# Conv-FFN stage of a streaming encoder layer on one core: first adds ahead of weight splits, normalising spread over two periods, token loads moved at block changes

## The reference

```
up = h @ w_up                       # 1024 -> 2 x 2816
ext = concat([conv_hist, up])
c = ext[0:T]*w_dw[0] + ext[1:T+1]*w_dw[1] + ext[2:T+2]*w_dw[2] + b_dw
a, b = split(c, 2)
ffn = (silu(a) * b) @ w_down        # 2816 -> 1024
x2 = LayerNorm(ALPHA*x1 + ffn + sigmoid(x1 @ w_pg) * (p @ w_pe))
```

## Time and profile before

| | |
|---|---|
| median of 3 runs | 3041.18 us (3038.22 to 3047.57) |
| the profiled execution: time, span | 3045.18 us, 3043.4 us |
| TensorE / VectorE / ScalarE / GpSimd busy | 94% / 69% / 48% / 35% |
| ffn stage | from 1446 us to the end |
| mean granted TensorE clock | 0.970 |

### The profile page before, as it was taken

One profiled execution on the slowest core, in us unless ns is written; L12 is line 12 of the kernel. 1 busy time (PEld: TensorE's weight loads), 2 busy tenths in 40 slices (PEclk: granted clock), 3 DMA queues, 4 the chain that ended last, 5 costly groups with the idle time before them and its releaser, 6 DMA issues. The chain is left out here.

```text
span 3043.4 us, 47351 instructions
## 1 busy us (share of the span) xinstructions
PE 2853.6 (94%) x14597; PEld 2481.4 (82%) x14597; DVE 2110.9 (69%) x3081; ACT 1451.0 (48%) x2947; POOL 1066.3 (35%) x816
## 2 busy tenths in 40 slices
PE   8998999999999899999899999988999997999996
PEld 6877787777777688887798988878999996888885
DVE  5635776777776444445687877797777778788776
ACT  4342555877787222222453444443544544455553
POOL 5341544766676433334433333210111111111113
PEclk9997998999999999999999999989999998999998
DMA  4226452222113333334633324344323334533331
GB/s 136 87 69 145 139 167 56 43 62 47 43 43 129 129 104 103 103 103 147 206 108 103 118 91 133 116 142 161 100 93 117 100 94 137 183 121 119 107 119 58
DMA packets 234859, 333.26 MB, mean 110 GB/s; under 512 B 66897, under 2 KB 109617, under 8 KB 233361
## 3 DMA queue, kind: packets, MB, share of 16 engines
q1 hardware_dynamic: 234736, 331.76, 35.5%
HBM read 246.05 MB, written 85.63 MB: 109 GB/s over the span
## 5 line engine op out<-in xcount | busy, mean ns | idle before, releaser
L3053 DVE TENSOR_TENSOR mx_w_lo<-ff_w_raw,mx_w_hi 128x512 fp32r<-128x512 f32 x390 | 312.3, 827 | 23.8 <-ACT mx_w_hi L2867 23.7
L2767 POOL TENSOR_TENSOR mx_odd<-ff_d_raw,mx_odd 128x512 fp32r<-128x512 f32 x66 | 91.5, 1386 | 596.1 <-ACT mx_odd L2876 595.4
L2867 ACT ACTIVATE mx_w_hi<-ff_w_raw 128x512 fp32r<-128x512 f32 x390 | 232.7, 622 | 33.9 <-POOL ff_w_raw L2755 33.9
L3110 DVE TENSOR_TENSOR ho_raw<-ho_raw,ff_d 128x512 f32<-128x512 f32 x264 | 168.3, 681 | 114.4 <-PE ff_d L86 110.0
L1567 POOL TENSOR_TENSOR at_p_lo<-at_p,at_p_hi 128x512 fp32r<-128x512 f32 (+2 forms) x160 | 187.6, 1173 | 164.1 <-ACT at_p_hi L1604 162.5
L2876 ACT ACTIVATE mx_odd<-ff_d_raw 128x512 fp32r<-128x512 f32 x66 | 41.5, 629 | 395.1 <-PE ff_d L86 389.7
L1597 ACT ACTIVATE at_p<-at_s 128x512 f32<-128x512 f32 (+1 forms) x320 | 169.9, 531 | 111.6 <-PE at_s L1793 56.4
L1709 DVE TENSOR_TENSOR at_p_lo<-at_p,at_p_hi 128x512 fp32r<-128x512 f32 (+1 forms) x160 | 187.3, 1171 | 45.2 <-ACT at_p_hi L1604 44.3
L84 PE MATMUL ff_d<-mx_odd,ff_h_hi 128*128 128x512 f32 x364 | 146.7, 403 | 40.5 <-DVE ho_raw L3110 30.2
L1604 ACT ACTIVATE at_p_hi<-at_p 128x512 fp32r<-128x512 f32 (+1 forms) x320 | 179.0, 560 | 0.0
L3086 DVE SCALAR_TENSOR_TENSOR ff_cv_a<-ff_up_a,ff_taps,ff_cv_a 128x768 f32<-128x768 f32 (+1 forms) x132 | 123.3, 934 | 55.5 <-ACT ff_cv_a L2933 28.2
(11 more groups left out here) (558 smaller groups left out, 9860.2 us busy)
## 6 DMA issues: line engine op xcount, KB each, us to landing
ff_w_raw<-in_w_ffn_p SPq DMA_DIRECT2D x216, 256.0 KB, 3.5
ff_w_raw<-scratch_sums SPq DMA_DIRECT2D x176, 256.0 KB, 3.5
ff_d_raw<-in_w_ffn_p SPq DMA_DIRECT2D x132, 256.0 KB, 2.8
scratch_sums<-ff_w_raw SPq DMA_DIRECT2D x84, 256.0 KB, 3.5
ho_raw<-in_x SPq DMA_DIRECT2D x17, 512.0 KB, 4.1
mx_m_raw<-scratch_mix_t SPq DMA_DIRECT2D x17, 512.0 KB, 5.2
scratch_x_t<-mx_work SPq DMA_DIRECT2D x17, 512.0 KB, 2.6
scratch_y<-mx_work SPq DMA_DIRECT2D x17, 512.0 KB, 2.9
```

Of the source, the lines that this page charges most:

```text
L2767: pool.tensor_tensor(lo, d_raw[:, :], f32(hi), ALU.subtract).then_inc(dlo, 1)
L2867: act.activation(w[j][0], raw, ACT.Copy).then_inc(whi, 1)
L3053: dve.tensor_tensor(w[j][1], raw, f32(w[j][0]), ALU.subtract).then_inc(wlo_dve, 1)
L3110: dve.tensor_tensor(y[t][:, H[i]], y[t][:, H[i]], ps_d[2 * (t % 2) + i][:, :], ALU.add)\
```

## The change

- **VectorE, block 0**: in even periods, the add of tile 0 goes ahead of the low of S2, that of tile 1 ahead of the low of S1, that of tile 2 ahead of the low of S3.
- **VectorE, block changes**: tiles 0 to 5 are normalised in periods 1 and 2 of the new block, none in period 0; the wait for y0 is one per tile.
- **VectorE and ScalarE, last period of a block**: B11 is split after join 2 and copy 2, not before them.
- **ScalarE**: the high of S4 goes from between copy 3 and `begin` 1 to after copy 0, ahead of the high of A22; at block changes the high of the last down piece goes up to right behind the silu; in periods 1 and 2 of blocks 1 and 2 copy 1 goes ahead of `product_hi`.
- **SP**: in a block's last period the loads of B11 and B21 go ahead of the load of down piece 2; stores and loads of y move with the normalising.
- **GpSimd**: rewritten, same order of instructions.

```diff
@@ sync @@
-                sp.dma_start(y[t], g["y0"][r:r + P, :]).then_inc(y_in, 16)
+                sp.dma_start(y[t], g["y0"][r:r + P, :]).then_inc(y_in[t], 16)
@@ even_loads @@
-                if turning:
-                    load_y(b, 3)
...
                 next_loads(b, f, p, 0, at_next, (A12,))
-                next_loads(b, f, p, 0, at_next, (S2, S1, S3))
+                if turning:
+                    store_y(b - 1, 3)
+                    store_y(b - 1, 4)
+                    load_y(b, 3)
+                next_loads(b, f, p, 0, at_next, (S2,))
+                if turning:
+                    load_y(b, 4)
+                    for t in range(5, BLOCKS[b - 1]):
+                        store_y(b - 1, t)
+                    for t in range(5, BLOCKS[b]):
+                        load_y(b, t)
+                next_loads(b, f, p, 0, at_next, (S1, S3))
                 load_down(b, p, at_d, 1)
@@ odd_loads @@
+                if turn:
+                    load_x(b + 1, B11)
+                    load_x(b + 1, B21)
                 load_down(b, p, at_d, 2)
                 for j in range(PRODUCTS):
-                    if turn and b < 2:
+                    if turn and j > 1:
                         load_x(b + 1, j)
@@ scalar, finish_up and period @@
                 copy(b, f, par, 3)
-                if nb < 3:
-                    weights(nb, nf, (S4,))
                 begin(b, f, p, i, 1)
...
                 if before is not None:
+                    weights(b, f, (S4,))
                     weights(b, f, (A22,), p, i)
                     activate(*before[:4])
+                if begins and b > 0:
+                    down_highs(before[0], before[2], (3,))
...
+                early = b > 0 and isinstance(f, int) and f in (1, 2)
+                if early:
+                    copy(b, f, i, 1)
                 if before is not None:
                     product_hi(*before[:4])
...
+                copy(b, f, i, 2)
                 if x_next:
                     tokens(b + 1, (B11,))
-                copy(b, f, i, 2)
@@ vector, add and period @@
+                if isinstance(p, int) and p == 0:
+                    dve.wait_ge(y_in[t], 16 * (b + 1))
...
                 join(b, f, par, 1)
+                join(b, f, par, 2)
                 if x_next:
                     tokens(b + 1, (B11,))
-                join(b, f, par, 2)
-                if more:
-                    weights(nb, nf, (S2,))
+                if b == 0 and par == 0 and adds is not None:
+                    add(*adds, 0)
+                weights(nb, nf, (S2,) if more else ())
...
+                if b == 0 and par == 0 and adds is not None:
+                    add(*adds, 1)
+                    weights(nb, nf, (S1,))
+                    add(*adds, 2)
+                    weights(nb, nf, (S3,))
+                    for t in range(3, BLOCKS[b]):
+                        add(*adds, t)
...
-                period(b, 0, 0, (b - 1, FT - 1, LAST, 1) if b else None, after_last=b > 0,
-                       norm=((), (), (0, 1)) if b else none)
+                period(b, 0, 0, 0, (b - 1, FT - 1, LAST, 1) if b else None)
-                period(b, 1, 1, (b, 0, 0, 0), norm=((2,), (3,), (4, 5)) if b else none)
-                period(b, 2, 0, (b, 1, 0, 1), adds=(b, 0))
+                period(b, 1, 0, 1, (b, 0, 0, 0), norm=((0, 1), (), (2,)) if b else none)
+                period(b, 2, 1, 0, (b, 1, 0, 1), adds=(b, 0), norm=((3, 4), (5,), ()) if b else none)
```

More of the change, by code:

```diff
@@ L2426, in ffn @@
         d_in = sem("d_in")
-        y_in, st_y, st_c = sem("y_in"), [sem(f"st_y{t}") for t in range(BLOCKS[0])], sem("st_c")
+        y_in, st_y = ([sem(f"{n}{t}") for t in range(BLOCKS[0])] for n in ("y_in", "st_y"))
+        st_c = sem("st_c")
         combined, whi = sem("combined"), sem("whi")
@@ L2682, in odd_loads @@
                         load_y(0, j - 1)
-                    if turning and b > 0 and 0 < j < 6:
-                        store_y(b - 1, j - 1)
-                        if j > 2:
-                            load_y(b, j - 3)
+                    if turning and b > 0 and j == 4:
+                        store_y(b - 1, 1)
+                        load_y(b, 0)
+                    if turning and b > 0 and j == 5:
+                        store_y(b - 1, 2)
+                        load_y(b, 1)
+                if turning and b > 0:
+                    load_y(b, 2)
             for j in (A11, A12, S1):
@@ L2794, in even @@
             def even(b, f, p):
+                begins = isinstance(f, int) and f == 0
+                if not begins:
+                    down_lows(b, p - 1, (3,))
                 if b == 0:
-                    if not (isinstance(f, int) and f == 0):
-                        down_lows(0, p - 1, (3,))
+                    if not begins:
                         pool.wait_ge(prod, per_f(0, f, PRODUCTS, S1))
@@ L2802, in even @@
                         combine(0, f + 2, p + 1, 0, (0, 1, 2))
[L2803 to L2812 removed]
+                if not at_end(b, p):
+                    down_lows(b, p, (0,))
+                if b == 0 and not (isinstance(f, int) and f == FT - 2):
+                    combine(0, f + 2, p + 1, 0, (3,))
             def odd(b, f, p):
[L2816 removed]
                 down_lows(b, p, (0, 1, 2) if at_end(b, p) else (1, 2))
[L2818 to L2820 removed]
             combine(0, 1, 0, 1)
             tokens(0, (T4,))
[L2824 to L2825 removed]
             for b in range(3):
@@ L2829, in _ @@
                     root(b - 1, range(BLOCKS[b - 1]))
-                    even(b, 0, 0)
-                    odd(b, 1, 0)
+                even(b, 0, 0)
+                odd(b, 1, 0)
                 with pool.Fori(0, LAST - 1) as q:
@@ L2939, in finish_up @@
             def finish_up(b, f, p, i, par):
-                nb, nf = following(b, f, 1)
                 begin(b, f, p, i, 0)
@@ L2994, in period @@
                     tokens(b, (T3,))
-                copy(b, f, i, 1)
+                if not early:
+                    copy(b, f, i, 1)
                 if i == 1:
                     down_highs(b, p, (1,))
-                elif before is not None:
+                elif before is not None and not begins:
                     down_highs(before[0], before[2], (3,))
@@ L3138, in normalise, with period @@
                        .then_inc(shifted, 1)
-            def period(b, f, par, before, adds=None, x_next=False, after_last=False, norm=((), (), ())):
+            def period(b, f, p, par, before, adds=None, x_next=False, norm=((), (), ())):
                 nb, nf = following(b, f, 1)
@@ L3156, in period @@
                         tokens(b, (T1,))
-                    weights(nb, nf, (A11, A12) if more else ())
+                    weights(nb, nf, (A11,) if more else ())
+                    weights(nb, nf, (A12,) if more else ())
                 else:
@@ L3165, in period @@
                     normalise(b - 1, norm[0])
-                if after_last:
+                if begins and b > 0:
                     tokens(b, (T3,))
@@ L3175, in period @@
                 join(b, f, par, 1)
+                join(b, f, par, 2)
                 if x_next:
                     tokens(b + 1, (B11,))
-                join(b, f, par, 2)
-                if more:
-                    weights(nb, nf, (S2,))
+                if b == 0 and par == 0 and adds is not None:
+                    add(*adds, 0)
+                weights(nb, nf, (S2,) if more else ())
                 if norm[1]:
                     normalise(b - 1, norm[1])
-                if par == 0:
-                    weights(nb, nf, (S1,) if more else ())
-                    if adds is not None and isinstance(adds[1], int) and adds[1] == 0:
-                        dve.wait_ge(y_in, 16 * (FIRST[b] + BLOCKS[b]))
+                if b == 0 and par == 0 and adds is not None:
[5 more added lines that the diff above has]
+                        add(*adds, t)
+                elif par == 0:
+                    weights(nb, nf, (S1,))
                     if adds is not None:
```

38 lines of the change are left out of this document (9 added, 29 removed).

## The result

The changed kernel takes **3004.12 us** (median of four runs, 3000.94 to 3005.70), the kernel before 3040.02 beside it: a ratio of **0.9878**, 95% interval 0.9863 to 0.9893, some 36 us faster by the medians. The forecast was 3012, the range 3000 to 3024.

The account below looks back on a forecast made before the run. TensorE's matmuls were taken to set the time, so only their waits could be won. Terms -23.2 + 1 - 5.9 - 1.6 + 0.8 = -28.9 gave 3016.3 on the profiled scale, 3012 as a median, range 3000 to 3024.

Parts of the forecast that it names:

- block 0 (-23.2 + 1): Block 0: ten TensorE waits for a pair's first add vanish, -23.2; S4's high uses up the 0.56 margin, +1.
- first change: Block 0 to 1: new block's first add 8.6 earlier, y0 wait of 4.26 dropped, low clock costs 2.7; sum -5.9.
- second change: Block 1 to 2: new block's first add 4.0 earlier, low clock at tile 2 costs 2.7; sum -1.6.
- block 2, S4's high: Block 2: TensorE's wait moves from S2 to S3, losing 0.1 eight times, +0.8.
- rival 2: Block changes give their waits, 12 each, by quicker VectorE lows or early T2: about 2996; chance 0.09.
- Old block's adds: Block change: VectorE reaches the old block's first add at 1998.0 where it was 2003.14, 5.1 earlier.
- Piece 2 behind the tokens: First block change: down piece 2, issued at 1969.8 behind 1.5 MB of tokens, lands at 1975.4.
- The wait of 5 for T2: Block change: TensorE still waits about 5 us for T2 before S2, which starts at 1986.8, not 1988.88.
- The stops of 8: Each block change: TensorE stops some 8 us at tile 2 because tiles 3, 4 and 5 are normalised first.
- Rival 3: Block 0: adds slowed beside GpSimd's S4 sum, ten waits stay, about 3034, no measurable change; chance 0.05.
- rival 4: Block 0: the sums' loop becomes the bound, each pair 4 longer at 12 late, about 3074; chance 0.03.
- Rival 1: Block changes give nothing, only block 0 counts: about 3020, or 3024 with both changes 2 us worse; chance 0.15.

Follow-up runs that it names:

- e12: The kernel before, unchanged, measured again for a second profile: ratio 0.9997 to the kernel before.
- e5: The changed kernel, unchanged, measured again: ratio 0.9868 to the kernel before, 3006.07 us.
- e1: Kernel before with only VectorE's block 0 adds moved up, plus a signal per tile for y0 and the rewritten GpSimd program: 3009.75 us, ratio 0.9882.
- e6: Changed kernel with S4's high back between copy 3 and the second begin: 3002.33 us, ratio 0.9857 to the kernel before.
- e3: Kernel before with only the block-end and next period 0 edits, plus a signal per tile for y0 and rewritten GpSimd program: ratio 0.9947.
- e7: Changed kernel with T2's load ahead of the load of down piece 3 at both block changes: ratio 0.9878 to the kernel before.
- e2: Kernel before with only S4's high moved behind copy 0, plus a signal per tile for y0 and rewritten GpSimd program: ratio 1.0031.
- e9: Changed kernel with S4's high back, tiles 4 and 5 normalised behind tile 3's add in period 2 and added mid period 3: 2994.92 us, ratio 0.9831.
- e4: Kernel before with only normalising spread over periods 1 and 2, y stores and reloads moved along, signal per tile, rewritten GpSimd program: ratio 0.9995.
- e10: Kernel before with two parts alone, the block 0 adds and the edits at block end and in period 0: ratio 0.9856.

## Why the prediction was right, and where it was off

Every sign that it named came: no wait for an add in block 0, A22 without a wait, S2 behind a wait of 4.27, stops of 7 at tile 2 with the lower clock behind them, and in block 2 less waiting for copy 0 and more for copy 1. The sum was short by about 8 us, and four steps came with a wrong price or a wrong reason: the waits of block 0, the wait for T2, the wait for y0, and S4's high.

| term | forecast | first profiles (before, after) | second profiles (e12, e5) |
|---|---|---|---|
| block 0 (-23.2 + 1) | -22.2 | -29.0 | -27.2 |
| first change | -5.9 | -7.7 | -10.0 |
| second change | -1.6 | -2.5 | -2.1 |
| block 2, S4's high | +0.8 | +2.1 | +2.3 |
| end | 0 | +0.3 | -1.3 |
| sum | -28.9 | -36.7 | -38.3 |

(Block 0: in the first profiles 26.6 up to the last downs and 2.3 of the last downs' own wait, which the table of stretches has in change 1; in the second 23.2 and 4.0.)

That the result still lies in the range, 4 us above its lower end, owes something to luck. The lower end was made of no low clock behind the stops, a better block 2 and an earlier T2. The low clock came, at 4.2 where 5.4 was counted, block 2 got worse, and T2 was not early; what pulled the time down, the price of the waits in block 0, was in no bound. The result is also as near to rival 2 (2996) as to the forecast; the stretches tell them apart, since each change was to give 12 by that rival.

- **Block 0.** "The wait goes, ten times: -23.2" took the listed waits for their whole cost. They cost 3.03 each and not 2.33, so e1's eight pairs won 24.2 where 18.6 was counted. This is the mis-sized term. It does not explain all of the 29.0: 1.5 of that lies ahead of the first downs, where the profiles scatter by 2.5 anyway. A sign of its price stood in the rows: in the same the first matmul behind the wait takes 0.50 where the others take 0.39, and the length of a pair of block 0 could have been set against one of block 1. That S4's high "uses up the margin" was right, and the +1 was small: the eight pairs are 1.8 and 3.1 longer than unbroken ones in the two profiles of the changed kernel, and 0.0 with S4's high back (e6).
- **Old block's adds.** With block 0's 29.0 and the stage's earlier start of 7.55 added to the times of the changed kernel (1949.70, 1955.56, 1960.98 and 2029.24), the forecast points came out within 0.6: S2 at 1986.8 forecast and 1986.2 found, the downs at 1992.1 and 1992.1, the first add of the old block at 1998.0 and 1997.5, that of the new block at 2066.2 and 2065.8. e3 alone shows the head's 5.0 and 4.0 for forecast 5.1 and 4.0.
- **Piece 2 behind the tokens.** It was issued at 1933.20 and its high began at 1938.69 after waiting for the DMA: 5.5, against 5.6 taken and 2.8 for the median piece. It landed 0.7 behind the second of the token loads that were issued ahead of it. This agrees with the rule cited from the Trainium skill (DMA: Bandwidth & Descriptors, Queues, rings and completion order).
- **The wait of 5 for T2** came (4.27), but its name was wrong: e7 shows ScalarE's queue, not the load, behind it.
- **"At the first change it drops the wait of 4.26 for y0, since tiles 0 and 1 are stored and reloaded a period earlier."** The wait went, for another reason: e1, e2 and e3 lose it with the old places. The line of the diff that did it, the signal per tile, had no term of its own. By its trace the new places alone would have made it worse, though no run shows it: in the changed kernel the y0 of tile 5 lands at 2037.96, 8.7 behind the first add at 2029.24, which would have waited for it under one signal.
- **The stops of 8** were 7.01 and 6.99, and VectorE's normalises made them: e9 took two away and the stop fell to 1.83. The lower clock cost 1.3 at the first change (12.52 against 11.22) and not 2.7; at the second 11.27 for three tiles that take some 8.3 unbroken (half of the 16.53 of six tiles), 2.9 more.
- **S4's high in block 2.** "silu comes 0.4 later and the gate 0.1" failed: copy 1 moved by the high's full 0.5. TensorE's wait for copy 0 fell by 2.9 and that for copy 1 rose by 3.6 in 320 us, and the matmuls behind pay as well: the seven pairs lost 2.1, where all of block 2 was to lose 0.8.
- **Rival 3** (adds slowed beside GpSimd): it did not come, the adds took 1.27 each beside the sums. The rule that the prediction cites from the Trainium skill (SBUF — State Buffer, Who interferes with whom) shows its other side here as well: at the first change the gate, with both inputs in SBUF, took 1.86 beside GpSimd's low of 2.08, where they take 0.96 and 1.30 alone. The trace agrees with the rule on both sides. **Rival 2** would have needed a faster T2, which e7 shows to bring nothing, and **rival 4** did not show. **Rival 1** was right that spreading the normalises gives nothing (e4, e10), and wrong that the head's gain would be eaten (e3).

## What to carry to other kernels

A wait in the middle of an otherwise full TensorE is worth more than the list of waits says: compare the length of the whole group with that of an unbroken one. One semaphore that counts several loads made the first consumer wait for the last load, though its own had landed 17 us before; look for the order in which they land before blaming where they are issued. When work is moved off one wait, put it where its engine idles *and* where nothing that another engine waits for stands behind it: the same two normalises cost 14 us ahead of a join, with late adds that waited for y0, and won 8 behind the adds.

## What the runs showed of the hardware

- Of waits of 2.0 to 2.6 in a TensorE that was busy before and after, some were followed by the lower clock level (matmul starts 0.42 apart, where 0.23) and some were not: two of block 0's ten downs groups in the first profile of before (20.73 and 21.00 long, clock 0.92) and three of ten in the second (20.50, 20.72, 20.92), the others 18.8 to 19.4 at 1.00. The length of the wait does not tell them apart: 2.02 and 2.28 were followed by it, 2.52 and 2.60 were not.
- A stop of 2.25 cost 0.29 beyond its length at full clock (16.82 against 16.53 busy for a group of 72 matmuls).
- A down piece of 256 KB that was issued behind two token loads of 768 KB was ready 5.5 after its issue, where the median piece takes 2.8. The twelve loads that SyncE issued between 1930.5 and 1942.9 in the changed kernel landed in the order of their issue.
